# First layer, output projection of the first tile: six of its eight steps between the memory heads' steps, or all eight in the output stage

## The chip, the cores and the metric

One core of one Trainium2 chip. The metric is the device time of one execution in microseconds (us); a kernel's time is the median of its runs. All data is float32.

## What is computed

One inference step of a decoder trunk with two layers, for 512 prompt tokens and 8 sample tokens that share all weights (width 1024). What matters here is the first layer's mixer and what follows it at once:

```
tok  = sigmoid(o) * mlstm(q, k, v, gates)            # 6 heads of 128: columns 0 to 767
m    = mem_attention(mq, mem_k, mem_v)               # 4 heads of 64:  columns 768 to 1023
mix  = concatenate([tok, m], axis=-1) @ w_out        # 1024 x 1024
x    = layer_norm(ALPHA * x + mix) * g + b
x    = layer_norm(ALPHA * x + hier_moe(x))
```

In `mem_attention` each token's query is scored against 256 memory rows, a softmax is taken, and the weights multiply the memory's values. For the prompt the memory is projected in the kernel; for the samples keys and values come from a cache.

## The kernel before, in words

The program is a sequence of blocks. In a block each engine has its own list of instructions, executed in order, with semaphores between the engines; at a block's end all engines meet. Tokens lie in five tiles: four of 128 prompt tokens and one (PT) with the 8 samples. `CAT` holds the concatenation, transposed, as eight slices of 128 columns (k = 0 to 7): slices 0 to 5 are the six mLSTM heads, slices 6 and 7 the memory heads. `WOUT0` holds `w_out` as two halves c of 512 output columns, each of eight slices k. One output of a tile and half is eight matmuls that add up in one PSUM bank; the trace has two records for each of these matmuls.

**The first block** makes the projections and the six mLSTM heads, and, beside and after the last head, the memory heads of the first layer. The end of TensorE's list (from line 724 on) is written out by hand:

```
pair_scores(1); turned_weights(0); turned_weights(1)
first_outputs(1)                       # 6 matmuls into bank 1
sample_scores(); pair_outputs(0, 7)
turned_weights(2); turned_weights(3)
sample_weights()
first_outputs(0)                       # 6 matmuls into bank 0
sample_outputs(); pair_outputs(1, 2); sample_features()
```

`pair_scores` makes the scores of two memory heads (L576). ScalarE then takes the exponentials (`softmax_of`, L771), VectorE normalises them (`normalize`, L965), `turned_weights` transposes them on TensorE (L585), ScalarE and VectorE copy the transposed weights out of PSUM (`turned_out`, L821 and L1017), and `pair_outputs` multiplies them by the memory's values (L594). The samples have a chain of their own: `sample_scores` (L606, which waits for both transposed-weight copies of VectorE of heads 0 and 1, since it writes bank 3), maximum on VectorE (L1025), exponentials on ScalarE (L835), `sample_weights` (transposes, L615), a copy on VectorE (L1031), `sample_outputs` (L626), two steps on VectorE (L1036), `sample_features` (L635), and a last copy into `CAT` (L1038). VectorE takes these in the order: copies of heads 0 and 1, maximum of head 3, `normalize(2)`, the samples' maximum, `normalize(3)`, copies of heads 2 and 3, the samples' copy, `sample_heads` (eleven small steps up to L943), L1033, L1036 twice, L1038. ScalarE takes: copies of heads 0 and 1, `softmax_of(2)`, `softmax_of(3)`, the heads' output of pair 0 (L825), the samples' exponentials, the copies of heads 2 and 3, the output of pair 1.

`first_outputs(c)` (L642) makes, for the first prompt tile alone, the six matmuls of half c that need only the mLSTM heads (k = 0 to 5), and leaves the bank's sum open.

**The output stage** (`output_and_norm`, the next block) takes the tiles in the order 0, PT, 1, 2, 3. TensorE makes each tile's output (L1181, and L1185 for the samples), VectorE adds the residual (L1243) and normalises, ScalarE takes the square root, TensorE transposes the result (L1088) and ScalarE copies it out (L1096). For tile 0 the loop over k begins at 6, since the rest was made before. SyncE issues at the block's start the loads of the norm's gain and bias (`GBM`), of two experts' weights and of the second layer's memory weights, then four more expert loads, and after the stage's last output matmul (`mm_ready`) two more. Then come the router, the experts, the combination, and the second layer, whose attention streams pages of a cache from HBM.

Of the kernel before, what the change touches and what calls it, by code (L numbers as in the profile page):

```python
# [21 lines left out]
P = 128  # L22
D = 1024
KC = D // P
# [6 lines left out]
H = 6  # L31
# [103 lines left out]
def build(nc, I, O, stop=None):  # L135
    ctx = ExitStack()
    with ctx:
# [296 lines left out]
        with nc.Block() as block:  # L434
            @block.sync
            def _(sp):
# [95 lines left out]
                sp.wait_ge(rest_in, 48)  # L532
                sp.wait_ge(smp_done, 1)
                sp.dma_start(X[0:NB, PT, :], I["xs"]).then_inc(xs_in, 16)

            @block.tensor
            def _(pe):
# [98 lines left out]
                                                    const("group_of"), start=True, stop=True)  # L636
                    last.then_inc(sf_ready, 2)

                def first_outputs(c):
                    pe.wait_ge(wo_in[c], 32 - 16 * c)  # L640
                    for k in range(H):
                        nc.tensor.matmul(PB[c][:, :], CAT[:, k, 0:P], WOUT0[:, c, k, :], start=(k == 0), stop=False)  # L642

                project(gate_unit)
                project(first_v)
                project(first_vs)
# [86 lines left out]
                pair_scores(1)  # L733
                turned_weights(0)
                turned_weights(1)
                pe.wait_ge(mt_act, 1)
                first_outputs(1)
                sample_scores()
                pair_outputs(0, 7)
                turned_weights(2)  # L740
                turned_weights(3)
                sample_weights()
                first_outputs(0)
                sample_outputs()
                pair_outputs(1, 2)
                sample_features()
# [392 lines left out]
        def output_and_norm(l):  # L1139

            with ExitStack() as st:
# [10 lines left out]
                with nc.Block() as block:  # L1152
# [17 lines left out]
                    def _(pe):  # L1170
                        if l == 1:
                            pe.wait_ge(wout_in, 32)
                        for i in range(NT + 1):
                            if i < NT:
                                t = order[i]
                                if i >= 2:
                                    pe.wait_ge(mm_used, m0 + i - 1)
                                for c in range(2):
                                    for k in range(H if l == 0 and i == 0 else 0, KC):
                                        if t < PT:  # L1180
                                            last = nc.tensor.matmul(PB[2 * (i % 2) + c][:, :], CAT[:, k, t * P:(t + 1) * P],  # L1181
                                                                    w_out(c)[:, k, :], start=(k == 0), stop=(k == KC - 1))
                                            continue
                                        for j in range(4):
                                            last = nc.tensor.matmul(PB[2 * (i % 2) + c][32 * j:32 * j + NB, 0:P], CAT[:, k, SEQ:TOK],  # L1185
                                                                    w_out(c)[:, k, j * P:(j + 1) * P], start=(k == 0), stop=(k == KC - 1))
                                last.then_inc(mm_ready, 1)
# [1774 lines left out]
```

## Time and profile before

| | |
|---|---|
| median of 3 runs | 1222.47 us (1221.97 to 1224.55) |
| the profiled execution | 1225.72 us |
| its span, first to last instruction | 1223.8 us |
| mean granted TensorE clock | 0.935 |
| busy: TensorE matmul / weight load | 1060.8 us (87%) / 641.7 us (52%) |
| busy: VectorE / ScalarE / GpSimd | 410.6 us (34%) / 261.5 us (21%) / 51.0 us (4%) |
| read from HBM, written | 288.31 MB, 29.97 MB |

All stretches below are in us from the span's start. A timeline row stands for several instructions of one line: the first one's start, the time from there to the last one's end, engine, line, operation, destination and source, shapes, count, and in brackets how long the engine was idle ahead of it and who ended that. Matmuls are pipelined and their ends are modelled, so that a matmul row runs on a little beyond the start of the next one; the starts are the firmer numbers.

### The profile page before, as it was taken

To read this page: it belongs to the slowest core of one execution; us is meant where nothing else is said; L and a number is where in the kernel's file an instruction comes from. 1 tells how busy PE (TensorE), PEld (TensorE's weight loads), DVE (VectorE), ACT (ScalarE), POOL (GpSimd) and SP (SyncE) were. 2 spreads that over 40 slices of the span, in tenths; PEclk is the share of its full clock that TensorE was granted. 3 is DMA by queue.
4 is the path that set the end of the run, shared out by engine and by line. 5 is a ranking of instruction groups with operands and counts; after the bars stand their busy time and mean duration, and the time that the engine had idled before them with its cause. 6 is when DMAs were issued, how large, how long until landed. Compare 5 with 4: busy or idle time off the path is not lost. (4 is left out here: it accounts for less than half of the span.)

```text
span 1223.8 us, 22941 instructions
## 1 busy us (share of the span) xinstructions
PE 1060.8 (87%) x9246; PEld 641.7 (52%) x9246; DVE 410.6 (34%) x1092; ACT 261.5 (21%) x688; POOL 51.0 (4%) x61
## 2 busy tenths in 40 slices
PE   7999999999989999449998978997877995999950
PEld 5888888865473333148875644453453444333210
DVE  3233323454453212180010143444442336321118
ACT  2222212131012111061110112333352001111114
POOL 0000000000000000200000000000010001000011
PEclk9999999999999999769999989999796997999985
DMA  7964323738448999999999928999643705899944
GB/s 235 291 234 127 118 64 87 273 116 305 179 180 339 392 422 355 321 359 324 362 344 350 352 87 310 354 355 364 235 122 121 310 35 220 329 360 406 388 157 173
DMA packets 128185, 319.80 MB, mean 261 GB/s; under 512 B 9679, under 2 KB 67200, under 8 KB 118606
## 3 DMA queue, kind: packets, MB, share of 16 engines
q1 hardware_dynamic: 116078, 275.03, 62.5%
q0 software_dynamic: 7504, 27.45, 6.3%
q10 hardware_dynamic: 4496, 15.83, 3.2%
q8 instruction: 75, 1.23, 0.4%
q14 instruction: 32, 0.26, 0.1%
HBM read 288.31 MB, written 29.97 MB: 260 GB/s over the span
## 5 line engine op out<-in xcount | busy, mean ns | idle before, releaser
L1566 PE MATMUL bank<-W,XT 128*32 128x512 f32 x1408 | 158.5, 603 | 5.6 <-DMA W<-in_w13f 3.0
L1181 PE MATMUL bank<-WOUT,CAT 128*128 128x512 f32 x232 | 101.4, 594 | 0.6 <-PEq L434 0.5
L561 PE MATMUL bank<-XT,WH 128*128 128x260 f32 x448 | 100.4, 384 | 0.0
L1566 PEld LDWEIGHTS bank<-W,XT 128*32 128x32 f32 x1408 | 44.0, 111 | 104.3 <-issue 100.6
L2408 PE MATMUL bank<-XT,W 128*64 128x260 f32 x768 | 92.5, 396 | 5.7 <-DVE CAT L2683 3.2
L561 PEld LDWEIGHTS bank<-XT,WH 128*128 128x128 f32 x448 | 84.4, 190 | 13.5 <-issue 0.3
L561 PE MATMUL bank<-WH,XT 128*128 128x256 f32 x384 | 84.8, 379 | 0.0
L1597 PE MATMUL bank<-WD,GT 128*32 128x512 f32 x704 | 80.0, 595 | 1.6 <-DVE GT L1671 1.6
L561 PEld LDWEIGHTS bank<-WH,XT 128*128 128x128 f32 x384 | 72.1, 190 | 9.8 <-issue 0.4
L2408 PEld LDWEIGHTS bank<-XT,W 128*64 128x64 f32 x768 | 55.5, 141 | 38.4 <-issue 9.2
L1181 PEld LDWEIGHTS bank<-WOUT,CAT 128*128 128x128 f32 x232 | 43.4, 190 | 52.8 <-issue 52.5
L1663 DVE TENSOR_TENSOR XT<-bank,XT 128x256 f32<-128x256 f32 x22 | 9.3, 424 | 140.8 <-ACT XT L1635 140.8
L2345 PE MATMUL bank<-PGS,CAT 128*32 128x384 f32 x512 | 49.6, 511 | 5.5 <-DMA PGS<-in_VP 5.5
L2254 PE MATMUL bank<-PGS,QD 128*32 128x128 f32 x1536 | 47.6, 275 | 4.7 <-DMA PGS<-in_KP 4.6
L2411 PE MATMUL bank<-WV,XT 128*128 128x256 f32 x192 | 46.8, 400 | 1.6 <-ACT XT L1096 1.6
L2254 PEld LDWEIGHTS bank<-PGS,QD 128*32 128x32 f32 x1536 | 40.5, 110 | 13.2 <-issue 10.6
L1597 PEld LDWEIGHTS bank<-WD,GT 128*32 128x32 f32 x704 | 20.8, 109 | 45.7 <-issue 43.7
L2411 PEld LDWEIGHTS bank<-WV,XT 128*128 128x128 f32 x192 | 37.6, 200 | 8.3 <-ACT XT L1096 1.7
L1088 PE MATMUL bank<-C,X 128*128 128x128 f32 (+1 forms) x120 | 16.9, 285 | 28.7 <-DVE X L1864 25.7
L1635 ACT ACTIVATE XT<-bank 128x256 f32<-128x256 f32 x22 | 8.5, 385 | 146.0 <-PE bank L1566 146.0
L1096 ACT ACTIVATE XT<-bank 128x512 f32<-128x512 f32 (+1 forms) x30 | 13.9, 515 | 89.6 <-PE bank L1088 89.6
L1088 PEld LDWEIGHTS bank<-C,X 128*128 128x128 f32 (+1 forms) x120 | 14.2, 156 | 35.2 <-DVE X L1864 26.6
(456 smaller groups left out, 1300.6 us busy)
## 6 DMA issues: line engine op xcount, KB each, us to landing
W<-in_w13f SPq DMA_DIRECT2D x32, 2048.0 KB, 12.7
PGS<-in_KP SPq DMA_DIRECT2D x128, 384.0 KB, 5.3
PGS<-in_VP SPq DMA_DIRECT2D x128, 384.0 KB, 5.3
WD<-in_w2f SPq DMA_DIRECT2D x32, 1024.0 KB, 15.3
WH<-in_w_a SPq DMA_DIRECT2D x13, 1024.0 KB, 10.0
WOUT<-in_w_out SPq DMA_DIRECT2D x3, 2048.0 KB, 10.9
YS<-CAT ACTq DMA_DIRECT2D x12, 512.0 KB
W<-in_w_b SPq DMA_DIRECT2D x6, 1024.0 KB, 11.2
```

The costliest lines, as they stand in the source:

```text
L561: last = nc.tensor.matmul(PB[u["bank"]][:, 0:u["w"]], u["lhsT"](w, k), u["rhs"](w, k), start=(k == 0), stop=(k == KC - 1))
L1088: last = nc.tensor.transpose(PB[4 + 2 * (n % turns) + k // 4][:, (k % 4) * P:(k % 4) * P + r], X[0:r, t, k * P:(k + 1) * P], const("ident" ...
L1096: last = nc.scalar.activation(XT[:, 4 * c:4 * c + 4, t * P:t * P + r], PB[4 + 2 * (n % turns) + c][:, :].rearrange("p (k n) -> p k n", k=4 ...
L1181: last = nc.tensor.matmul(PB[2 * (i % 2) + c][:, :], CAT[:, k, t * P:(t + 1) * P], w_out(c)[:, k, :], start=(k == 0), stop=(k == KC - 1))
L1566: last = nc.tensor.matmul(PB[2 + g % 2][32 * j:32 * j + 32, :], XGT[:, g % 2, k, 32 * j:32 * j + 32], W13[:, LANES[l][g][j] % WRING, k, :] ...
L1597: last = nc.tensor.matmul(PB[5 + c][32 * j:32 * j + 32, :], GT[:, g % 2, k, 32 * j:32 * j + 32], WD2[:, LANES[l][g][j] % WRING, k, c * 512 ...
L1635: nc.scalar.activation(SIL[:, g % 2, :], PB[2 + g % 2][:, 0:FE], ACT.Silu).then_inc(s_ready, 1)
L1663: nc.vector.tensor_tensor(GA[:, g % 2, :], PB[2 + g % 2][:, FE:2 * FE], SIL[:, g % 2, :], ALU.mult).then_inc(g_ready, 1)
L2254: last = nc.tensor.matmul(bank[32 * j:32 * j + 32, q * P:(q + 1) * P], QD[:, i, 4 * g + j, :], page[:, j, i, :], start=(i == 0), stop=(i = ...
L2345: last = nc.tensor.matmul(PB[6 + c][32 * j:32 * j + 32, 0:384], weight, v, start=(p == 0), stop=(p == PAGES))
L2408: last = nc.tensor.matmul(PB[u["bank"]][DM * m:DM * m + DM, 0:u["w"]], w[:, k, at:at + DM], u["rhs"](w, k), start=(k == 0), stop=(k == KC ...
L2411: last = nc.tensor.matmul(PB[u["bank"]][0:u["m"], 0:u["w"]], u["lhsT"](w, k), u["rhs"](w, k), start=(k == 0), stop=(k == KC - 1))
```

## The change

The two calls of `first_outputs` and the function go away, with the wait of TensorE for `mt_act` ahead of the first of them. The output stage makes all eight steps of tile 0 in both halves, as it does for the other tiles. The waits for the halves of `w_out` (`wo_in`), which stood in `first_outputs`, now stand at the end of SyncE's list in the first block.

```diff
@@ -532,6 +532,8 @@
                 sp.dma_start(X[0:NB, PT, :], I["xs"]).then_inc(xs_in, 16)
+                sp.wait_ge(wo_in[0], 32)
+                sp.wait_ge(wo_in[1], 16)
@@ -635,11 +637,6 @@
-                def first_outputs(c):
-                    pe.wait_ge(wo_in[c], 32 - 16 * c)
-                    for k in range(H):
-                        nc.tensor.matmul(PB[c][:, :], CAT[:, k, 0:P], WOUT0[:, c, k, :], start=(k == 0), stop=False)
@@ -733,14 +730,11 @@
                 turned_weights(1)
-                pe.wait_ge(mt_act, 1)
-                first_outputs(1)
                 sample_scores()
                 pair_outputs(0, 7)
                 turned_weights(2)
                 turned_weights(3)
                 sample_weights()
-                first_outputs(0)
                 sample_outputs()
@@ -1176,7 +1170,7 @@
                                 for c in range(2):
-                                    for k in range(H if l == 0 and i == 0 else 0, KC):
+                                    for k in range(KC):
```

## Rows read from the trace of the kernel before

**Rows 1.** The page's first part: busy time, share and instructions of each engine.
```profile
PE 1060.8 (87%) x9246; PEld 641.7 (52%) x9246; DVE 410.6 (34%) x1092; ACT 261.5 (21%) x688; POOL 51.0 (4%) x61
```

**Rows 2.** Timeline of TensorE, from the first of the moved steps to the output stage.
```profile
258.66 5.39 PE L642 MATMUL bank<-WOUT,CAT 128*128 128x512 f32 x12
263.98 1.93 PE L606 MATMUL bank<-QK,XT 128*32 128x256 f32 x32
265.85 1.94 PE L594 MATMUL bank<-MEMT,MEMV 128*64 128x512 f32 x8
267.72 1.97 PE L585 MATMUL bank<-C,SO 128*128 128x128 f32 x16
269.52 0.64 PE L615 MATMUL bank<-C,XT 128*128 128x128 f32 x4
270.00 5.32 PE L642 MATMUL bank<-WOUT,CAT 128*128 128x512 f32 x12
275.24 0.41 PE L626 MATMUL bank<-QK,XT 128*32 128x256 f32 x2
...
277.11 1.94 PE L594 MATMUL bank<-XT,MEMV 128*64 128x512 f32 x8
278.97 1.05 PE L635 MATMUL bank<-C,XT 128*128 128x4 f32 x8
280.55 3.67 PE L1181 MATMUL bank<-WOUT,CAT 128*128 128x512 f32 x8 [0.52 <-PEq L434]
284.15 3.68 PE L1185 MATMUL bank<-WOUT,CAT 128*8 128x128 f32 x128
287.87 14.00 PE L1181 MATMUL bank<-WOUT,CAT 128*128 128x512 f32 x32
```

**Rows 3.** Timeline of VectorE over the same stretch.
```profile
258.37 1.28 DVE L1017 COPY MEMT<-bank 128x512 f32<-128x512 f32 x2
...
261.53 1.14 DVE L965 TENSOR_SCALAR SO<-SO,MX 128x256 f32<-128x256 f32 x4
265.99 0.69 DVE L1025 TENSOR_REDUCE SX<-bank 128x2 f32<-128x512 f32 x1 [3.32 <-PE bank L606]
...
267.07 1.14 DVE L965 TENSOR_SCALAR SO<-SO,MX 128x256 f32<-128x256 f32 x4
...
270.33 0.68 DVE L1031 COPY XT<-bank 128x512 f32<-128x512 f32 x1
...
273.72 0.16 DVE L1033 RECIPROCAL SX<-SX 128x2 f32<-128x2 f32 x1
...
286.53 1.29 DVE L1243 SCALAR_TENSOR_TENSOR X<-X,bank 128x512 f32<-128x512 f32 x2 [5.89 <-DMA GBM<-in_ln_mix_b]
```

**Rows 4.** Timeline of ScalarE: pair 0's output and the samples' second exponential.
```profile
267.94 0.60 ACT L825 ACTIVATE CAT<-bank 128x512 f32<-128x512 f32 x1 [4.83 <-PE bank L594]
...
268.88 0.47 ACT L835 ACTIVATE XT<-bank,SX 128x256 f32<-128x256 f32 x1
```

**Rows 5.** DMA issues from 250 to 290: size and us to landing.
```profile
WOUT<-in_w_out SPq DMA_DIRECT2D x1, 1024.0 KB, 5.7
```

**Rows 6.** TensorE's timeline at the output stage's end.
```profile
334.82 1.97 PE L1088 MATMUL bank<-C,X 128*128 128x128 f32 x8 [2.94 <-DVE X L1074]
```

**Rows 7.** Windows: busy us of PE, PEld, DVE, ACT, POOL, then PEclk, DMA share, GB/s.
```profile
320.00:340.00 20.00, 17.05 (x58) 9.51 (x57) 10.07 (x16) 2.53 (x6) 0.00 (x0) 0.85 0.41 154
340.00:360.00 20.00, 16.90 (x132) 14.06 (x130) 8.93 (x40) 2.66 (x7) 0.00 (x0) 0.98 0.34 135
...
400.00:420.00 20.00, 20.00 (x184) 6.41 (x180) 3.52 (x7) 2.44 (x5) 1.77 (x2) 1.00 0.99 379
```

**Rows 8.** Waits of SyncE's queue from 480 to 560: total us, times, longest.
```profile
SPq L2198 <- ACT LNSF L1815: 6.3, 2, 4.5
```

**Rows 9.** Windows of 2 us, columns as in Rows 7.
```profile
354.00:356.00 2.00, 1.29 (x8) 1.11 (x9) 1.61 (x10) 0.00 (x0) 0.00 (x0) 1.00 0.00 0
...
876.00:878.00 2.00, 0.85 (x8) 0.61 (x7) 1.86 (x8) 1.11 (x4) 0.00 (x0) 0.69 0.09 37
```

## The prediction

> **What bounds the kernel now.** I began with the page's first part: TensorE is busy for 87% of the span, no other engine for half as long [rows 1]. So the question in any stretch is first whether TensorE is at work there or waits. The second view is TensorE's timeline over the stretch that the change touches [rows 2]. From 258.66 to 280.0 each group begins where the one before it ends; the only idle time named is 0.52 us at the meeting of the engines between the two blocks. The output stage then goes from 280.55 to 287.87 and on without a wait named. TensorE sets the pace through this whole stretch, and it works through its list in order: when the head of the list waits, nothing behind it is taken.
>
> The third view is what the other two engines do meanwhile [rows 3, 4]. Each step of the memory heads needs something from VectorE or ScalarE, and in the kernel before those results lie ready, because TensorE spends 5.3 us on the first group of moved steps (258.66 to 263.98) and 5.2 us on the second (270.00 to 275.24) [rows 2]. The moved steps are thus filling in two places where TensorE would otherwise be early. That is what has to be priced.
>
> **The change, part by part.** *The matmuls themselves.* 12 matmuls, 24 records, leave the first block. They took (263.98 - 258.66) + (275.24 - 270.00) = 5.32 + 5.24 = 10.56 us [rows 2]. The same 24 records come back in the output stage, where 32 of them take 14.00 us with the last one's tail, 0.4375 us each at most, so 10.4 to 10.5 us [rows 2]. Moving alone is worth -0.1 us. The first tile and half no longer reopen a bank that was left unfinished; nothing in the rows prices that, and its two sides are the 0.44 us per record of the moved groups and the 0.45 us of the eight records from 280.55 to 284.15, so at most 0.2 us either way. I take nothing.
>
> *The first place: between the transposes of head 1 and the samples' scores.* `sample_scores` writes bank 3 and waits for VectorE's second copy. The two copies start at 258.37 and last 1.28 us, so they end at 259.65 [rows 3]. TensorE would be there at 258.66 and waits until about 259.75 with the hand-over (the step from L594's end, 265.85 + 1.94 = 267.79, to L825's start at 267.94 was 0.15 [rows 2, 4]). **Gap 1.1 us.** Then the scores take 265.85 - 263.98 = 1.87 us to 261.6, and pair 0's outputs 267.72 - 265.85 = 1.87 us to 263.5 [rows 2].
>
> *The second place: transposes of heads 2 and 3.* Those of head 2 need `normalize(2)`, done at 261.53 + 1.14 = 262.67 [rows 3]: no wait, 0.9 us (half of 269.52 - 267.72 [rows 2]), to 264.4. Those of head 3 need `normalize(3)`, which stands on VectorE behind `normalize(2)` and the samples' maximum. From the maximum's start to the end of `normalize(3)` it was 267.07 + 1.14 - 265.99 = 2.22 us [rows 3]; now it starts at 262.6 and ends at 264.85. **Gap 0.5 us**, and the transposes run to 265.8.
>
> *The third place: between `sample_weights` and `sample_outputs`, where the second filling was.* The exponentials are in time: pair 0's output ends on TensorE at 263.5, ScalarE starts L825 at 263.7, and the second exponential ends 0.94 + 0.47 us later, at 265.1 [rows 4]. `sample_weights` runs from 265.8 to 266.3 (270.00 - 269.52 = 0.48 [rows 2]). VectorE can copy head 3's weights only from 265.9, 0.64 us, and then the samples' transposed weights, 0.68 us [rows 3], so that TensorE gets them at about 267.3. **Gap 1.0 us.**
>
> *The fourth: before `sample_features`.* From `sample_outputs` to there TensorE needs 278.97 - 275.24 = 3.73 us, to 271.05 [rows 2]. VectorE has its copy start at 266.55; to the end of the reciprocal behind `sample_heads` it was 273.72 + 0.16 - 270.33 = 3.55 us [rows 3], so 270.1, and two diagonal steps more, estimated from their kind at half a microsecond each, reach 271.1. **Gap 0.1 us.** What the first filling covered is thus the copies, what the second covered is VectorE's queue; late next is always VectorE.
>
> *The end of the block.* From `sample_features` on everything is as before: 280.55 - 278.97 = 1.58 us, so the output stage starts at 272.7 instead of 280.55, 7.8 us earlier. Then tile 0 needs 10.4 to 10.5 us more. The sum is +2.6 us (the four gaps, 2.7, less 0.1).
>
> *SyncE.* Two waits are added at the end of its list. Behind them stands nothing in the block, and who waits is the meeting of the engines. The last load they wait for takes 5.7 us to land [rows 5] and its queue place is unchanged, well over 10 us ahead of the block's end; they come after an issue that waits for `sample_heads`, which is done at about 270. Cost zero, covered by `sample_features`; with that cover gone it would be a few hundredths. The loads of the output stage are issued 7.8 us earlier. Their one visible customer is the first residual step, which waited for the gain and bias until 286.53 though tile 0's output was there at 284.2 [rows 2, 3]. Now tile 0 is done at 272.7 + 14.0 = 286.7 and the load is long in: the step starts 0.3 us later than before instead of 2.6, but VectorE has room there and the later tiles wait for TensorE, so this gains nothing. The two expert loads behind `mm_ready` go 2.6 us later with TensorE.
>
> *Does the delay reach the end?* After the output stage TensorE waits 2.94 us for the last but one norm [rows 6], a chain that itself hangs on TensorE's last output and transposes; it shifts as a whole. In the experts TensorE is busy 20.00 of 20.00 us [rows 7], so nothing is made up. The page stream of the second layer waits, at its start, for the norm after the experts (the 6.3 us of L2198 [rows 8]), so it shifts too. I find no slack that would take the 2.6 us.
>
> The profiled execution goes from 1225.72 to 1228.3 (span 1223.8 to 1226.4). It stood 3.25 us above the median of 1222.47; on the median that gives **1225.1 us**.
>
> **The rivals.** *A: part of it is absorbed.* The gaps come out shorter (each hangs on hand-overs that I read at 0.1), or the last tile's chain gives some back: the clock fell there, and the means 0.85 and 0.98 of two 20 us windows are 20 x 0.15 + 20 x 0.02 = 3.4 us of lost clock [rows 7]. If the shifted stretch keeps its clock, up to all of that is saved. For it: spread of the runs, 2.6 us. Against it: that fall follows an idle time that the change leaves. Time 1221.7 to 1224.6, middle 1223.5: no change that can be told.
>
> *B: the clock falls in the thinned-out stretch.* Now TensorE works there at a granted clock of 1.00. After the change some 2 us around 266 to 268 would be only half filled, and transposes before that. In the rows a 2 us window with 1.29 us busy kept the clock at 1.00, one with 0.85 us busy did not (0.69, so from 2.4 to 1.2 GHz within it) [rows 9]. Ours, with a gap of 1.0 us, lies between them. A fall costs as the one above, up to 3.4 us [rows 7], taken as 1.7 to 3.4: 1226.8 to 1228.5 us, middle 1227.7. The Trainium skill, in "TensorE: Matmul & The Clock Gate", section "Why this matters for your kernels", says that the clock drops after idle gaps much longer than any of these four; by that B would not happen and the time would stay at the forecast's. The window with 0.85 us busy speaks against relying on that, so B keeps a chance.
>
> *C, the other sign: the output stage hangs on its loads, not on TensorE.* If what follows is set by the loads that start with the block, all of it starts 7.8 us earlier: 1222.5 - 7.8 = 1214.7 us. For it: the first residual step did wait for such a load [rows 3]. Against it: TensorE went on through 284.15 and 287.87 without waiting [rows 2]. It decides only if the first residual step's start, and not the last output matmul, sets the stage's end; the loads would have to be waited for by 2.6 us more than TensorE is.
>
> **How the numbers follow.** A measurement of this kernel can tell about 0.2%, 2.4 us, from no change; the forecast's 2.6 us stands almost on that line. Forecast 0.52, of which 0.33 over the line and 0.19 under it; A 0.24 (0.22 same, 0.02 faster by the runs' spread); B 0.19 (0.17 slower, 0.02 same); C 0.05, faster. Together slower 0.50, same 0.43, faster 0.07. The range leaves out C and the ends of A and B: 1222.3 to 1228.3.
>
> **What would show it.** L642 gone; 32 records of L1181 for the first tile, about 14 us; the samples' scores start near 259.75 behind a wait for VectorE of about 1.1 us; gaps of about 0.5 and 1.0 us behind L585 and L615; the output stage starts at 272.7; the samples' tile follows near 286.7; the first expert matmul and everything after it 2.6 us later. The forecast is wrong if TensorE shows no idle time between 258.7 and 271, if the stage's start moves by other than 7 to 8.5 us, or if a clock below 1.00 stands between 259 and 287.

## Result and profile after

The changed kernel is slower, by more than was forecast. Over 20 runs of each the median is **1231.62 us** (1222.63 to 1237.69) against **1225.53 us** (1220.82 to 1228.87) for the kernel before; ratio 1.0053, 95% interval 1.0035 to 1.0071. The prediction was 1225.1 us, with a range to 1228.3. Two things are in the miss. The 1222.47 us from which the forecast counted is the median of three runs that came out low: beside the changed kernel the same program took 1225.53, which is 3.1 us of the 6.5. The rest is the change: 6.1 us by these medians, where 2.6 were forecast. The 6.1 are themselves uncertain (the ratio's interval is 4.3 to 8.7 us); 92 runs with the same order of work, given below, put the change at 4.2 us.

The profiled execution took 1234.05 us, at a mean granted clock of 0.933 over a span of 1232.1 us. The page's first part:

```profile
PE 1061.3 (86%) x9246; PEld 643.4 (52%) x9246; DVE 410.0 (33%) x1092; ACT 261.3 (21%) x688; POOL 50.7 (4%) x61
```

TensorE is busy as long as before (1061.3 against 1060.8 us [rows 1]): nothing was added to its work, and the span is 8.3 us longer than the profiled one of before, so the loss shows as time in which TensorE idles (these two spans are single executions; how far two such can differ by themselves is shown below). What happened where the change was made stands in TensorE's timeline, columns as in [rows 2]:

```profile
256.53 1.97 PE L587 MATMUL bank<-C,V 128*128 128x128 f32 x16
259.47 1.93 PE L608 MATMUL bank<-QK,XT 128*32 128x256 f32 x32 [0.97 <-DVE MEMT L1011]
261.33 1.94 PE L596 MATMUL bank<-MEMT,MEMV 128*64 128x512 f32 x8
263.20 1.09 PE L587 MATMUL bank<-C,SO 128*128 128x128 f32 x8
264.52 1.09 PE L587 MATMUL bank<-C,SO 128*128 128x128 f32 x8 [0.23 <-DVE SO L959]
265.45 0.60 PE L617 MATMUL bank<-C,XT 128*128 128x128 f32 x4
267.04 0.41 PE L628 MATMUL bank<-QK,XT 128*32 128x256 f32 x2 [0.99 <-DVE XT L1025]
...
268.90 1.94 PE L596 MATMUL bank<-XT,MEMV 128*64 128x512 f32 x8
270.77 1.05 PE L637 MATMUL bank<-C,XT 128*128 128x4 f32 x8
272.35 13.97 PE L1175 MATMUL bank<-WOUT,CAT 128*128 128x512 f32 x32 [0.52 <-PEq L434]
286.25 3.68 PE L1179 MATMUL bank<-WOUT,CAT 128*8 128x128 f32 x128
289.86 14.00 PE L1175 MATMUL bank<-WOUT,CAT 128*128 128x512 f32 x32
```

L642 is gone. Three waits for VectorE stand where TensorE never waited before. The brackets give 0.97, 0.23 and 0.99 us, counted from the modelled ends; by starts, which are firmer, the same places cost 1.14 us (259.47 - 256.53 = 2.94 against 1.80 for 16 such records without a wait, 269.52 - 267.72 [rows 2]), 0.45 us (265.45 - 263.20 = 2.25 against the same 1.80) and 1.11 us (267.04 - 265.45 = 1.59 against 270.00 - 269.52 = 0.48 [rows 2]). Tile 0's output is now 32 records in 286.25 - 272.35 = 13.90 us, 10.30 more than before. So 1.14 + 0.45 + 1.11 + 10.30 = 13.00 us come in and 10.56 go out: +2.44 us at the end of tile 0's output.

VectorE over the same stretch, columns as in [rows 3]:

```profile
258.04 1.28 DVE L1011 COPY MEMT<-bank 128x512 f32<-128x512 f32 x2
...
262.25 0.68 DVE L1019 TENSOR_REDUCE SX<-bank 128x2 f32<-128x512 f32 x1
263.32 1.14 DVE L959 TENSOR_SCALAR SO<-SO,MX 128x256 f32<-128x256 f32 x4
...
265.65 0.69 DVE L1011 COPY XT<-bank 128x512 f32<-128x512 f32 x1 [0.59 <-PE bank L587]
266.26 0.68 DVE L1025 COPY XT<-bank 128x512 f32<-128x512 f32 x1
...
269.84 0.88 DVE L1030 SCALAR_TENSOR_TENSOR XT<-bank,SX,C 128x256 f32<-128x256 f32 x2
...
286.46 1.28 DVE L1237 SCALAR_TENSOR_TENSOR X<-X,bank 128x512 f32<-128x512 f32 x2 [14.03 <-PE bank L1175]
```

The scores wait for the copies that end at 259.32; head 3's transposes wait for `normalize(3)`, which ends at 264.46, behind the samples' maximum; `sample_outputs` waits for the copy that ends at 266.94. These are the three releases that the prediction named. The first residual step waits for TensorE and no longer for the gain and bias (5.89 us for `GBM` in [rows 3]).

**The measure used from here on.** Two traces can be laid side by side from any common mark. I take two issues of SyncE: the store of `MEMV` in the middle of the last head, before the change has touched anything, and the two expert loads behind `mm_ready`, the last output matmul of the stage. SyncE's timeline of the kernel before,

```profile
254.00 0.41 SPq L190 DMA_DIRECT2D out_mem_v<-MEMV  x1
...
331.03 0.81 SPq L1128 DMA_DIRECT2D W<-in_w13f  x2
367.64 0.39 SPq L1276 DMA_DIRECT2D out_mem_k<-XT  x1
```

and of the changed one:

```profile
253.67 0.41 SPq L190 DMA_DIRECT2D out_mem_v<-MEMV  x1
...
333.01 0.80 SPq L1122 DMA_DIRECT2D W<-in_w13f  x2
```

That is 77.03 and 79.34 us: **+2.31 us** at the end of the output stage. I call it the stage's interval. (It is a little less than the 2.44 us at tile 0's end: the samples' tile behind it takes 289.86 - 286.25 = 3.61 us, and took 287.87 - 284.15 = 3.72 [rows 2].) The eight traces in which these steps stand as before (with edits elsewhere or none) give 76.94 to 77.08, the eight of the changed order 79.34 to 79.36. Locally the change cost nearly what was forecast (2.6), and always the same. Everything unexpected lies behind this point. The third line shown of before, SyncE's store of the second layer's memory keys (`out_mem_k`, called the store of `MEMK` from here on), is the mark used for the stretch that follows.

### The profile page after: what moved, and what is told of

Read it like the earlier page. It is cut to its first block and busy times, and to the rows that moved or that the text cites. A ratio compares the mean times of both kernels' runs of the same rounds, so it can differ in the third digit from the quotient of the medians.

```text
span 1232.1 us, 22942 instructions
## 1 busy us (share of the span) xinstructions
PE 1061.3 (86%) x9246; PEld 643.4 (52%) x9246; DVE 410.0 (33%) x1092; ACT 261.3 (21%) x688; POOL 50.7 (4%) x61
## 5 line engine op out<-in xcount | busy, mean ns | idle before, releaser
L1175 PE MATMUL bank<-WOUT,CAT 128*128 128x512 f32 x256 | 111.7, 594 | 0.5 <-PEq L434 0.5
L1175 PEld LDWEIGHTS bank<-WOUT,CAT 128*128 128x128 f32 x256 | 48.0, 190 | 58.4 <-issue 58.4
```

## The experiments

A kernel's time scatters from run to run: over the 195 runs of the kernel before that stood beside these experiments its standard deviation is 3.2 us, about 0.26%. So besides each ratio I give, where it decides, the difference of means against all 195 (mean 1226.1), with a 95% interval, and pool kernels that share the order of TensorE's work. `after` and `before` below mean the two kernels of the case.

### Each half alone

The kernel before with one of its two fillings taken out:

```diff
-                first_outputs(0)                          # e1: half 1 stays early
+                for k in range(H if l == 0 and i == 0 and c == 1 else 0, KC):
```
```diff
-                first_outputs(1)                          # e2: half 0 stays early
+                for k in range(H if l == 0 and i == 0 and c == 0 else 0, KC):
```

Each has one wait at the end of SyncE's list in place of the one in `first_outputs`.

> Only the second of the two moved groups goes to the output stage (half 1 keeps its six early steps, half 0 does not). Gap theory: the first waiting place stays filled, the one ahead of the samples' outputs opens (about 1.0 us), so the output stage's last matmul ends about 1.0 us later than in the kernel before, and the whole time rises by 1 us if the shift passes through unchanged, to about 1226.5. If the measured 6 us come from something tied to the move of the work itself (loads that start earlier, the first tile's output in one piece), about half of them, 3 us, appear here. Clock theory (falls made likelier by the thinned-out stretch): near the kernel before, within 1 us, since the longest thin part is broken by dense matmuls.

> Only the first of the two groups is moved (half 0 keeps its six early steps, half 1 does not). Gap theory: the gaps ahead of the samples' scores (1.0 us) and between the two transposes (0.2 us) open, the last stays filled; +1.2 us at the output stage's end and about that at the end of the kernel. The two halves alone must add up to the 2.3 us of the changed kernel at that place, and if time is only passed on, to 2.3 us at the end as well.

Measured: e1 1226.82 us, ratio 1.0018 (0.9993 to 1.0043); e2 1227.89 us, 1.0023 (1.0005 to 1.0040). The stage's interval is 331.31 - 253.37 = 77.94 us in e1, 0.9 more than before, and 331.57 - 253.27 = 78.30 in e2, 1.3 more. Together 2.2, against 2.31 with both: the two places add up. Each gap came back alone as it stands in the changed kernel: TensorE's timeline of e1,

```profile
268.89 0.64 PE L616 MATMUL bank<-C,XT 128*128 128x128 f32 x4
270.48 0.41 PE L627 MATMUL bank<-QK,XT 128*32 128x256 f32 x2 [0.95 <-DVE XT L1031]
```

and of e2:

```profile
259.07 1.93 PE L607 MATMUL bank<-QK,XT 128*32 128x256 f32 x32 [0.98 <-DVE MEMT L1016]
...
264.13 1.09 PE L586 MATMUL bank<-C,SO 128*128 128x128 f32 x8 [0.23 <-DVE SO L964]
```

The times rise by 1.3 ± 2.5 and 2.3 ± 1.5 us. That fits one or two microseconds and is too coarse to say more.

### The loads held, and the gaps filled

Two things that the change does besides waiting were taken away. In e3 SyncE issues the output stage's loads only when tile 0's first half is made, about where they started before; in e5 the two gaps of a microsecond are filled: one superfluous matmul of `CAT` by `WOUT0`, of two records, stands ahead of `sample_scores` and one ahead of `sample_outputs`, into a bank that is overwritten later (they add work and no result). The first one also brings two waits that it needs itself, for `mt_act` and for `WOUT0`'s half; the lines below leave them out.

```diff
+                        if l == 0: sp.wait_ge(held, 1)                        # e3, on after: SyncE, head of the stage
+                        if l == 0 and i == 0 and c == 0 and k == KC - 1: last.then_inc(held, 1)
```
```diff
+                nc.tensor.matmul(PB[1][:, :], CAT[:, 0, 0:P], WOUT0[:, 1, 0, :], start=True, stop=True)   # e5, twice
```

> The changed kernel, with the output stage's loads held back until half 0 of its first tile is made, so that they start at about 280 as in the kernel before instead of at 272. If the earlier loads cost time (they meet other traffic, or set a later queue in another order), the time falls back by up to 3.8 us, to within 2.5 us of the kernel before. If they do not matter, it equals the changed kernel: about 6 us over the kernel before.

> The changed kernel with one superfluous matmul (two records, 0.9 us) in each of its two longest gaps, so that TensorE works there without delaying what follows by more than 0.1 us. Gap theory: the gaps stay as places where time is lost, so the output stage begins where it does in the changed kernel and the whole time is the changed kernel's, whatever that is above the kernel before. Clock theory (in a share of the runs the thin stretch brings the clock down and that makes up the rest over 2.3 us): the fall goes away and the time returns to about 2.4 us over the kernel before, and the spread of the runs to that of the kernel before.

Measured: e3 1229.99 us, ratio 1.0040 (1.0020 to 1.0059); e5 1231.35 us, 1.0036 (1.0016 to 1.0056). Against all runs of before that is +3.5 ± 1.7 and +4.9 ± 1.8 us. Neither brought the time back, and neither changed the stage's interval (79.36 and 79.35). The fillings did stand in the gaps; e5's timeline of TensorE:

```profile
258.37 1.10 PE L735 MATMUL bank<-WOUT,CAT 128*128 128x512 f32 x2
259.51 1.93 PE L608 MATMUL bank<-QK,XT 128*32 128x256 f32 x32
...
265.93 1.02 PE L741 MATMUL bank<-WOUT,CAT 128*128 128x512 f32 x2
```

So a clock that falls in the thinned stretch is not what costs: with the gaps filled the time stayed, and its interval leaves out the local 2.3 us. For the loads that start 8 us sooner e3 alone doesn't decide, since its interval (1.8 to 5.2) holds both 2.3 and 4.2; the next experiment, in which they stay where they were, does more. In the windows from 259 to 287 the granted clock is 1.00 in every trace, filled or not.

### The same delay without the change

If the surplus came from anything particular to the new order, a plain delay of the same size at the same place should cost only itself. The kernel before, with three superfluous matmuls at the head of the output stage, which write a bank that is overwritten later (run twice, e4 and g2):

```diff
+                        else:                                 # layer 0
+                            for k in range(3):
+                                nc.tensor.matmul(PB[2][:, :], CAT[:, k, P:2 * P], w_out(0)[:, k, :], start=True, stop=True)
```

> The kernel before with three superfluous matmuls (six records, 2.6 us, dense) at the head of the output stage: a pure shift of all that follows by 2.6 us, with no gap, no thin stretch and no load moved. If a shift is passed on as it is: +2.6 us at the end. If the stages behind make more of a shift than it was (the rise from 2.3 us at the output stage to 6 us at the end): about +6 us. If the clock's falls in the thin stretch are the rest: +2.6 us here and more only in the changed kernel.

> The kernel before with three superfluous matmuls at the head of the output stage, once more: a pure shift of 2.5 us. Its first twelve times lay 4.7 us (give or take 2.1) over the kernel before at a mean granted clock of 0.9323, against 0.9350. If a shift brings the clock down more often by itself, both come again (4 us and more, a clock of 0.933 or less). If that was chance, the twenty-four together come to 2.5 to 3.5 us and the clock to 0.934.

Measured: e4 1231.77 us, ratio 1.0030 (1.0008 to 1.0052); g2 1230.90 us, 1.0032 (1.0005 to 1.0058). TensorE in e4:

```profile
279.60 2.81 PE L1175 MATMUL bank<-WOUT,CAT 128*128 128x512 f32 x6 [0.52 <-PEq L434]
282.25 3.60 PE L1184 MATMUL bank<-WOUT,CAT 128*128 128x512 f32 x8
```

They put 2.65 us in, and the stage's interval is 79.49 us, +2.5. Together their 24 runs are **4.8 ± 1.5 us** above the kernel before. All kernels with the changed order (the changed kernel, e3, e5, e6, f2, f4, f6: 92 runs, stage's interval +2.3) are **4.2 ± 0.8 us** above it. This is the experiment that decides most: a delay with no new waits, no new order of loads and no gap costs, within the intervals, what the change costs. So the surplus of some 2 us over the local cost needs nothing of the change but the delay at this place. The margin is narrow for e4 and g2: set only against the runs of before that stood beside each of them, they come to 4.4 ± 1.8 us, which just leaves out the 2.5 that were put in. The changed order comes to 4.4 ± 0.9 in this way.

### Both kernels again

> The changed kernel once more, unchanged, for a second trace and for twelve more times. If its rise is the 2.3 us found at the output stage and the rest chance: +2 to +4 us here, with the surplus of its trace in other stages than in the first one. If the surplus is the change's own: +6 us again, and in the same stages (ahead of the combination, in the page stream).

> The kernel before once more, for a second trace. Against its own runs: 0 within about 1.5 us. If the stages in which the two first traces drift apart (the last output store of the experts, the page stream, the end) vary as much between two traces of this one kernel, their difference there isn't the change's. If they agree with the first trace of before within 0.5 us each, it is.

Measured: e6 1231.27 us, ratio 1.0025 (1.0003 to 1.0047); e7 1224.90 us, 0.9993 (0.9974 to 1.0012). The changed kernel keeps its level of 1231; the kernel before does so too, at 1225 and not at the 1222.5 of the first three runs. The two traces of before differ more than a few tenths: from the end of the output stage to the store of `MEMK` just ahead of the experts it is 367.64 - 331.03 = 36.61 us in one and 364.41 - 330.57 = 33.84 in e7,

```profile
330.57 0.81 SPq L1128 DMA_DIRECT2D W<-in_w13f  x2
364.41 0.40 SPq L1276 DMA_DIRECT2D out_mem_k<-XT  x1
```

and only the first shows the clock fall there that [rows 7] holds. The windows of e7, columns as in [rows 7]:

```profile
320.00:340.00 20.00, 17.06 (x96) 10.45 (x95) 9.97 (x15) 2.64 (x6) 0.00 (x0) 1.00 0.43 165
340.00:360.00 20.00, 16.90 (x108) 14.01 (x107) 11.39 (x52) 2.66 (x7) 2.05 (x2) 1.00 0.36 133
```

A row thus tells of one execution: the same stretch of the same program can lie 2.8 us apart, which is also what the fall in that trace costs (the prediction took 3.4 from the windows' means). In the five other traces with one fall (e3, e6, f1, f5, f8) the stretch takes 35.4 to 35.5 us. The changed order, in the windows of the changed kernel and of g2:

```profile
320.00:340.00 20.00, 17.06 (x54) 8.94 (x53) 10.03 (x16) 2.48 (x6) 0.00 (x0) 0.92 0.31 115
340.00:360.00 20.00, 16.90 (x120) 13.92 (x119) 10.42 (x39) 2.33 (x7) 0.00 (x0) 0.93 0.43 175
```
```profile
320.00:340.00 20.00, 17.06 (x57) 9.11 (x56) 10.12 (x15) 2.53 (x6) 0.00 (x0) 0.91 0.31 116
340.00:360.00 20.00, 16.90 (x118) 13.93 (x116) 10.15 (x39) 2.27 (x6) 0.00 (x0) 0.91 0.42 174
```

Here the clock is below 1.00 in both windows. Their traces show two separate falls, near 337 and near 357; so do e5, f4 and f6, while e6 and e3 show one and f2 none (g2 has its two near 336.0 and 356.5). Of the six traces of the order of before (before, e7, f1, f3, f5, f8) four show one fall there and two none. Over the seven traces of the changed order this stretch is 36.2 us in the mean, over those six 35.1. That is a hint of one more microsecond, from few traces.

### SyncE's two waits

The prediction priced these at zero. In f1 and f5 the kernel before gets nothing but the two waits; in f2 and f6 the changed kernel has them on TensorE's list behind `sample_features` and not on SyncE's; f8 is the kernel before with four waits, all long satisfied.

```diff
+                sp.wait_ge(wo_in[0], 32)                     # f1, f5: on before; f8: two more, for the samples' cache
+                sp.wait_ge(wo_in[1], 16)
```
```diff
-                sp.wait_ge(wo_in[0], 32)                     # f2, f6: on after
-                sp.wait_ge(wo_in[1], 16)
+                pe.wait_ge(wo_in[0], 32)                     # behind sample_features()
+                pe.wait_ge(wo_in[1], 16)
```

> The kernel before, with nothing of the change but its two waits at the end of SyncE's list in the first block. In all traces whose SyncE list carries these two, SyncE issues the last expert load 0.3 us sooner after TensorE than in the others, and where no matmuls are added besides, the last prefetch of the second layer's weights is all issued 1.1 us ahead of the experts' last output store, which then lands 8.1 to 8.2 us after its issue instead of 5.5. If SyncE's list is what shifts this: store to landing about 8 us here, and 1 to 3 us more than the kernel before at the end. If it is the order of TensorE's work: 5.5 us, and no difference.

> The kernel before with the two waits on SyncE, once more. The first trace of it had the experts' last store land 8.3 us after its issue, against 5.5 in three traces without the waits, but its twelve times (+1.4 us, give or take 2.2, against all runs of the kernel before) fit both a full passing-on of these 2.8 us and none. If the later landing is the program's own, it is 8.1 to 8.3 us again; if it is passed on to the end, the twenty-four times together lie 2 to 3 us over the kernel before; if later stages absorb it, within 1 us.

> The changed kernel with its two waits at the end of TensorE's list in the first block instead of SyncE's, so that SyncE's list is that of the kernel before. The output stage's end stays 2.3 us late. If SyncE's list sets the surplus: the last store lands 5.5 to 7 us after its issue and the whole is 2.5 to 4 us over the kernel before. If it doesn't: 8.1 us, and 5 us over it.

> The changed kernel with its waits on TensorE's list, once more. The store lands after 6.8 us again, and the output stage is 2.4 us late. Passed on in full: 24 times together 3.7 us over the kernel before (2.4 + 1.3), and 1.3 us under the changed kernel as it is. If only the output stage's delay counts: 2.4 us over.

> The kernel before with four satisfied waits at the end of SyncE's first list. If it is the length of SyncE's list that decides in which order its prefetches and the store meet, the pattern changes with it: one wait left the last expert load at 15.45 us ahead of the store, two and three moved it to 15.8. With four either the same 15.8 (a threshold) or back to 15.45 (a place in some unit of the list). The landing follows the prefetch: 8 us where that is all issued 1 us ahead of the store, 5.5 to 7 where it ends behind it.

Measured: f1 1227.70 us, 1.0001 (0.9975 to 1.0026); f5 1225.15 us, 0.9992 (0.9975 to 1.0009); f8 1227.03 us, 1.0005 (0.9986 to 1.0025). The 36 runs together: +0.3 ± 1.1 us. f2 1227.10 us, 1.0012 (0.9985 to 1.0040); f6 1230.03 us, 1.0051 (1.0028 to 1.0075); together +3.7 ± 1.7, which fits the 4.2 of the changed order. f2 alone seemed to give the loss back; its repetition f6 took that away. The waits show no cost in time, to about a microsecond.

They are not without trace, though. The experts' last store of results (`YS`) is waited for by ScalarE, and how long it takes to land depends on whether the last prefetch of the next layer's weights (`W<-in_w_b`) is issued before it. ScalarE's timeline of before, of the changed kernel, and of f5:

```profile
503.35 0.34 ACTq L1629 DMA_DIRECT2D YS<-CAT  x1
...
508.85 0.20 ACT L1750 ACTIVATE SW<-SW 1x1 f32<-1x1 f32 x1 [5.63 <-DMA YS<-CAT]
```
```profile
505.87 0.34 ACTq L1623 DMA_DIRECT2D YS<-CAT  x1
...
514.04 0.20 ACT L1744 ACTIVATE SW<-SW 1x1 f32<-1x1 f32 x1 [8.29 <-DMA YS<-CAT]
```
```profile
500.96 0.34 ACTq L1631 DMA_DIRECT2D YS<-CAT  x1
...
509.15 0.20 ACT L1752 ACTIVATE SW<-SW 1x1 f32<-1x1 f32 x1 [8.32 <-DMA YS<-CAT]
```

And SyncE's last two prefetches in before, the changed kernel and f1:

```profile
494.81 8.95 SPq L2176 DMA_DIRECT2D W<-in_w_b  x2
```
```profile
496.92 7.90 SPq L2170 DMA_DIRECT2D W<-in_w_b  x2
```
```profile
492.50 7.84 SPq L2178 DMA_DIRECT2D W<-in_w_b  x2
```

In before the second prefetch is all issued at 494.81 + 8.95 = 503.76, behind the store's start (503.35), and the store lands in 5.5 us. In the changed kernel, e3, e6, f1 and f5 it is all issued 1.1 us ahead of the store, which then takes 8.1 to 8.3 us. In the fifteen other traces the second prefetch follows the store by 0.1 to 0.6 us, and the landing is 5.2 to 7.2. So two waits that never wait move an issue 240 us later by 1.5 us and a landing by 2.7, and both are the program's own, the same in f1 and f5; four waits (f8) and the fillings (e5, g1) tip the order back, the issue at 0.1 to 0.3 us behind the store. And yet f1 and f5 take the time of before (+0.3 ± 1.3 us): what the store loses there is not passed on to the end. Where it is made good the runs don't say; what follows is the page stream.

### The last prefetch held

If the late landing cost time, holding the fourth prefetch until the results are stored should gain it back, in either kernel:

```diff
+                    if n == 3:                                # f3 on before, f4 on after
+                        sp.wait_ge(y_out, 2 * NG)
```

> The kernel before, with the last of the four weight prefetches issued beside the experts held until the last output has been copied for its store. The store's packets then have one load less ahead of them. Queue theory: store to landing falls from 5.5 to about 4 us, the combination begins 1 to 1.5 us sooner, and the whole is 1 us under the kernel before unless the held load is then waited for by TensorE (it would be seen ahead of the samples' projections, at 530). If the landing does not depend on the loads: 5.5 us and no gain.

> The changed kernel with the same prefetch held. Queue theory: its surplus goes with the queue, store to landing falls from 8.1 to the same value as in the kernel before with this edit, and against that kernel it is 2.3 us slower, the delay at the output stage alone; against the kernel before about +1 us. If the surplus has another cause, it stays 5 us over the kernel before.

Measured: f3 1223.58 us, ratio 0.9980 (0.9953 to 1.0006); f4 1229.19 us, 1.0022 (0.9994 to 1.0050). f4 did to its trace what it should:

```profile
505.81 0.34 ACTq L1623 DMA_DIRECT2D YS<-CAT  x1
...
511.05 0.20 ACT L1744 ACTIVATE SW<-SW 1x1 f32<-1x1 f32 x1 [5.37 <-DMA YS<-CAT]
```

The landing goes from 8.2 to 5.2 us, and the time is still 3.4 ± 2.4 us above the kernel before. That interval holds the local 2.3 as well as the 4.2, so f4 alone leaves the store open. What speaks against it is f1 and f5, where the same late landing left the time at +0.3 ± 1.3, and e4 and g2, whose stores land in 6.7 to 6.9 us and which cost as much as the change. f3's landing stayed at 5.4, as it was, so its -1.8 ± 1.3 us, if it is more than chance, does not come from where the expectation put it.

### A dense filler where TensorE waits

The fall near 335 follows a wait of 2.94 us for the norm [rows 6]. One part of what comes later needs no norm: the second layer's projection of memory for n = 2. In e8 (on before) and g1 (on after) its eight matmuls of half a bank stand in that wait and leave the place behind the router (the counts of the semaphores go down by one with them):

```diff
+                            if l == 0 and i == NT:            # TensorE, ahead of the last but one norm's transposes
+                                pe.wait_ge(mm_used, m0 + NT - 1); pe.wait_ge(mem1_w, 32); pe.wait_ge(mem1_x, 16)
+                                for k in range(KC):
+                                    last = nc.tensor.matmul(PB[3][:, 256:512], MEMT1[:, k, 0:P], WM1[:, 1, k, :],
+                                                            start=(k == 0), stop=(k == KC - 1))
+                                last.then_inc(early, 1)
...
+                                nc.scalar.activation(MEMV[:, 1, 0, :], PB[3][:, 256:512], ACT.Copy).then_inc(early, 1)
...
-                    memory(2)
```

f7 is e8 with the held prefetch of f3.

> The kernel before with one of the four pieces of the second layer's memory projection (3.6 us of dense matmuls) moved from the stretch ahead of the experts into the 2.9 us for which TensorE waits at the output stage's end. Two gains if the reading is right: the clock does not fall at 334, so the router's matmuls run at the full clock (about 1.5 us net of the 0.7 us by which the piece is longer than the gap), and 3.6 us less stand ahead of the first expert, of which the gather's landing lets through about 2.4 us. Together 3 to 4 us under the kernel before. If a shift at this place is passed on amplified, 6 us or more; if later stages absorb it, less than 2.

> The kernel before with both edits that alone lay under it: a piece of the second layer's memory projection in TensorE's wait at the output stage's end (-3.4 us, give or take 2.0) and the last weight prefetch held until the last output is copied (-1.7, give or take 1.4, with the landing at 5.4). If they add up: 4 to 5 us under the kernel before. The store would land after 5.2 to 5.5 us, against 6.8 with the first edit alone, and that difference of 1.4 us is what holding the load is worth here.

> The changed kernel with the piece of memory projection in TensorE's wait at the output stage's end, where the clock fell at 337 in its traces and a second time at 357 in several. Against the same edit on the kernel before (3.3 us under the kernel before, give or take 2.0) the delay of the output stage remains, 2.35 us. If the clock's falls ahead of the experts make up what the changed kernel loses beyond that, the two kernels with this edit differ by 2 to 3 us and no more, so this one is 0 to 2 us under the kernel before, with no fall between 330 and 350. If the surplus sits elsewhere, they differ by 5 us and this one is 1 to 2 us over it.

Measured: e8 1223.04 us, ratio 0.9963 (0.9938 to 0.9987); f7 1221.73 us, 0.9967 (0.9950 to 0.9984); g1 1225.95 us, 0.9995 (0.9972 to 1.0017). e8's timeline of TensorE:

```profile
329.48 1.04 PE L1088 MATMUL bank<-C,X 128*128 128x128 f32 x8
330.36 3.62 PE L1194 MATMUL bank<-WM,MEMT 128*128 128x256 f32 x16
333.81 1.04 PE L1088 MATMUL bank<-C,X 128*128 128x128 f32 x8
334.78 5.82 PE L1204 MATMUL bank<-XT,WR 128*20 128x128 f32 x64
...
361.36 1.09 PE L1566 MATMUL bank<-C,CAT 128*128 128x128 f32 x8 [1.01 <-DMA CAT<-XN,IDX]
```

The wait is gone, the router's 64 records take 5.82 us, as they do in the traces without the fall (e7, f2), and not 7.70 as in the trace of before or 6.58 as in the changed one, and the stretch from the stage's end to the store of `MEMK` is 30.67 or 30.68 us in e8, f7 and g1. g1's first window confirms it: no idle time, and no fall.

```profile
320.00:340.00 20.00, 20.00 (x81) 11.97 (x80) 9.94 (x16) 2.94 (x8) 0.00 (x0) 1.00 0.31 113
```

Not all of what the stretch gives is kept: from the store of `MEMK` to the experts' last store of results (`YS`) it is 135.70 or 135.71 us in all 17 traces without the filler, 136.31 in e8 and g1, and 137.82 in f7, where the granted clock is 0.91 in the window from 360 to 380 and 1.00 in e8's.

By means: e8 -3.5 ± 2.0, f7 -4.4 ± 1.5, the two together -3.9 ± 1.3 us: a version faster than both kernels of the case. g1 lies 4.5 ± 1.8 us under the changed kernel, so the filler gains there as much.

g1 was meant for more. Without a fall of the clock between 320 and 350, and with the stretch to the store of `MEMK` equally long in all three, the changed order should cost just its 2.3 us if the surplus sat in those falls. Measured is g1 over e8 and f7: 4.4 ± 1.9 us. The interval reaches down to 2.5, but the middle is where it was without the filler. The falls ahead of the experts are thus not shown to be the surplus.

## Why the prediction was wrong, point by point

**The gaps: right.** Forecast were 1.1, 0.5, 1.0 and 0.1 us. By starts they are 1.14, 0.45 and 1.11, each behind the instruction of VectorE that was named, and none at `sample_features` (270.77 - 268.90 = 1.87 us, as before). The last hung on two diagonal steps estimated at half a microsecond each; they take 0.44 each (0.88 for the two at L1030) and end at 270.72, just in time for 270.77. e1 and e2 gave the two places back one at a time.

**The moved matmuls: right, slightly low.** Forecast -0.1 us, measured 10.30 - 10.56 = -0.26. The output stage starts at 272.35 for 272.7, and 7.87 us earlier by the common mark for the 7.8 forecast. Sum at its end: +2.6 forecast, +2.31 measured, and within 0.1 us of that in every trace of this order.

**The loads: right.** By the common mark the first residual step starts 0.26 us later (286.46 - 253.67 against 286.53 - 254.00), forecast 0.3, and it waits for TensorE. That their earlier start costs nothing at the end is not shown by e3 alone; e4 and g2, with the loads where they were, lose as much as the change. Rival C, in which everything follows them, did not occur.

**SyncE's waits at zero: right for the time** (+0.3 ± 1.1 us over 36 runs), though not for the reason given alone. "Behind them stands nothing in the block" was true, and still the following issues shifted: in the traces with two or more of them the last expert load and the first prefetch go out 0.33 us sooner relative to the store, and in five of these traces the last prefetch 1.5 us. The prediction had no term for an order of issues that tips over.

**"I find no slack", and the 2.6 us pass to the end as they are: this is the step that failed,** in the direction that was not priced. The prediction treated what follows as rigid: 2.6 in, 2.6 out, or something absorbed (rival A). It had no case in which a delay grows. The 92 runs of the changed order say 4.2 ± 0.8 for 2.3 put in; the 24 of e4 and g2 say 4.8 ± 1.5 for 2.5. None of the signs by which the prediction wanted to be found wrong came true (no idle time in the first block, a stage's start moved by other than 7 to 8.5 us, a clock below 1.00 between 259 and 287): all of them watched the local part, none what follows it. Rival A is thereby refuted: more comes out than went in, whether the change or dead matmuls make the delay.

**What the surplus is, as far as the runs tell.** It goes together with a lower mean granted clock over the whole run: 0.9336 ± 0.0005 in the changed order and 0.9325 ± 0.0012 in e4 and g2, 0.9350 ± 0.0004 in before. From run to run of one kernel 0.001 of that mean goes with about 1 us of time; at equal clock the changed order is 2.8 ± 0.6 us above before, close to the local 2.3. So about 1.4 of the 4.2 us goes with the clock. That is a correlation: a run that waits more also has more falls, and the runs don't say which leads. In the traces the one visible place is ahead of the experts (36.2 against 35.1 us in the mean, the fall near 357); g1, which has no fall between 320 and 350, did not lose the surplus. It is not in the experts of the first layer, which take the same 135.7 us with and without the delay. Where the rest sits, whether in the page stream or elsewhere in the second layer, **stays open**: those stretches vary from trace to trace by more than is sought (from the first issue of a K page to the first of a V page it is 160.1 us in before and 162.9 in e7, and 156.8 to 163.8 over all twenty).

**Rival B** named the clock, which may have a part in the surplus (about 1.4 us goes with it), and the wrong place. Between 259 and 287 the clock was 1.00 everywhere, in spite of gaps of a microsecond, and filling them changed nothing. The Trainium skill ("TensorE: Matmul & The Clock Gate", section "Why this matters for your kernels") names much longer idle gaps as what makes the clock drop; in this stretch the trace agrees, with gaps of 1.14 us at most. At the fall near 357 in the changed kernel the trace does not agree, and the measurement decides: from 346 to the fall TensorE was never idle for longer than 1.38 us, between groups of small matmuls, and the granted clock is 0.83 in the window from 356 to 358 and 0.50, the level of 1.2 GHz, in the next.

**The base.** The forecast added its difference to a median of three runs. With a standard deviation of 3.2 us from run to run such a median is uncertain by some 2 us, about as much as the whole effect; the profiled execution, at 1225.72, stood nearer to the median of 195 runs (1225.9) than those three did. That alone put 3.1 us between forecast and result, and with the true base the forecast, 1228.5, would have missed by 3.1.

## What to carry to other kernels

Work that fills an engine's wait is worth the wait that it covers: price its removal by what the other engines still owe at that moment, queue by queue, and the local sum comes out to a few tenths. A local sum is not yet a time: the same microseconds inserted as dead weight at the same spot are the cheapest test of what the rest of the program makes of them (here 4.8 ± 1.5 us for 2.5), and it takes dozens of runs, since one trace or a median of three scatters as widely as the effect. The largest wait ahead of a stage of small matmuls (here 2.94 us) was here a good place for independent work: filling it gave 3.9 ± 1.3 us, about as much as both early halves had.

## What the runs showed of the hardware that was not expected

- **A fall of the clock in one execution of a program and none in the next.** The stretch behind the output stage took 36.61 us in one execution of the kernel before, with a granted clock of 0.85 in the window from 320 to 340, and 33.84 us in another, with 1.00.
- **Filling a wait returned its length, and the fall of the clock behind it.** Eight matmuls moved into a wait of 2.94 us shortened the stretch to the store of `MEMK` by 3.2 us against a trace without the fall, and by 5.9 against one with it; in all three traces with the filler it lasts 30.67 or 30.68 us. The stretch behind it was 0.6 us longer in two of them and 2.1 us in the third.
- **The landing of a store depends on the order of issue against a neighbour's load.** With the load 1.1 us ahead the 512 KB store landed in 8.1 to 8.3 us, with the load just behind in 5.2 to 7.2, and no more than some 1.5 us of the difference reached the end of the program (+0.3 ± 1.3 in the 24 runs of f1 and f5).
- **Two satisfied waits on one engine's list** shifted the issue of a load 240 us later by 0.33 us in every trace that had them, and that of the last prefetch by 1.5 us in some, with +0.3 ± 1.1 us in the time.
